# A chunked state-space scan: running sums made once and spread by DMA, decays made one head pair ahead

## The reference, cut to what matters

```python
acs = jnp.cumsum(dt * a.reshape(G, R), axis=2)          # running sums inside chunks of 128
xdt = x * dt[..., None]
seg = at[..., :, None] - at[..., None, :]               # at = acs with time last
decay = jnp.exp(jnp.where(causal, seg, -jnp.inf))       # 128 x 128 per head and chunk
cb = jnp.einsum('bctgn,bcsgn->bcgts', cm, bm)
y_diag = jnp.einsum('bcgrts,bcsgrp->bctgrp', cb[:, :, :, None] * decay, xdt)
decay_s = jnp.exp(acs[:, :, -1:] - acs)
states = jnp.einsum('bcsgn,bcsgr,bcsgrp->bcgrpn', bm, decay_s, xdt)
...
y_off = jnp.einsum('bctgn,bcgrpn,bctgr->bctgrp', cm, h_in, jnp.exp(acs))
```

## Time and profile before

| | before |
|---|---|
| median of 3 runs | 2653.37 us (2649.86 to 2658.57) |
| span of the profiled execution | 2654.9 us (its own time is not listed apart from the span) |
| TensorE matmul / weight load | 2539.5 us (96%) / 2452.5 us (92%) |
| VectorE | 1279.4 us (48%) |
| ScalarE | 728.7 us (27%) |
| GpSimd | 532.4 us (20%) |
| instructions | 46230 |
| bytes read / written in HBM | 207.20 MB / 14.49 MB |

### The profile page before, as it was taken

One profiled execution on the slowest core, in us unless ns is written; L12 is line 12 of the kernel. 1 busy time (PEld: TensorE's weight loads), 2 busy tenths in 40 slices (PEclk: granted clock), 3 DMA queues, 4 the chain that ended last, 5 costly groups with the idle time before them and its releaser, 6 DMA issues.

```text
span 2654.9 us, 46230 instructions
## 1 busy us (share of the span) xinstructions
PE 2539.5 (96%) x18319; PEld 2452.5 (92%) x18319; DVE 1279.4 (48%) x1499; ACT 728.7 (27%) x1016; POOL 532.4 (20%) x388
## 2 busy tenths in 40 slices
PE   7999999898989879999999999999999999999997
PEld 7999999887878668999999999999998989999997
DVE  5434334778677776343433244434325635344323
ACT  4222222321212223222222232222224533222212
POOL 1000022456556552300000210000123222000021
PEclk9999999999999888999999999999999979999999
DMA  3222224122232221222222222222222102222222
GB/s 121 83 83 79 88 87 137 56 89 90 90 101 93 82 73 62 79 86 81 79 87 85 89 80 79 86 80 79 90 93 89 40 26 80 87 79 82 85 89 81
DMA packets 61268, 220.47 MB, mean 83 GB/s; under 512 B 7120, under 2 KB 7248, under 8 KB 61056
## 3 DMA queue, kind: packets, MB, share of 16 engines
q1 hardware_dynamic: 52560, 187.72, 20.8%
q0 software_dynamic: 8368, 31.59, 3.9%
q10 hardware_dynamic: 288, 0.44, 0.0%
HBM read 207.20 MB, written 14.49 MB: 84 GB/s over the span
## 4 chain that ended last, share of the span: by engine, by line
PE 89%; DVE 5%; issue 3%; ACT 1%; DMA 1%; POOL 0%; DVEq 0%; ACTq 0%; POOLq 0%
PE psum L383 71%; PE psum L401 6%; PE psum L552 1%; PE psum L580 1%; DVE cacc L1192 1%; PE psum L666 1%; PE psum L573 1%; PE psum L548 1%; DVE xdd L1299 1%; PE psum L749 1%; PE psum L536 1%; PE psum L677 1%; PE psum L689 0%; PE psum L529 0%; DVE ylo L1413 0%
## 5 line engine op out<-in xcount | busy, mean ns | idle before, releaser
L1088 DVE TENSOR_TENSOR wlo<-wraw,whi 128x1024 fp32r<-128x1024 f32 x342 | 439.0, 1284 | 987.1 <-ACT whi L800 987.1
L383 PE MATMUL psum<-xhi,whi 128*128 128x288 f32 x3152 | 681.0, 298 | 21.9 <-DVE xlo L1094 15.1
L383 PE MATMUL psum<-xhi,wlo 128*128 128x288 f32 x3152 | 677.6, 297 | 0.0
L383 PE MATMUL psum<-xlo,whi 128*128 128x288 f32 x3152 | 677.5, 297 | 0.0
L800 ACT ACTIVATE whi<-wraw 128x1024 fp32r<-128x1024 f32 x349 | 369.8, 1059 | 973.0 <-PE psum L383 936.1
L383 PEld LDWEIGHTS psum<-xhi,whi 128*128 128x128 f32 x3152 | 510.8, 190 | 26.5 <-issue 21.9
L383 PEld LDWEIGHTS psum<-xlo,whi 128*128 128x128 f32 x3152 | 510.9, 190 | 0.0
L383 PEld LDWEIGHTS psum<-xhi,wlo 128*128 128x128 f32 x3152 | 510.4, 190 | 0.0
L383 PE MATMUL psum<-hhi,whi 128*128 128x288 f32 x1408 | 302.7, 296 | 0.0
L383 PE MATMUL psum<-hlo,whi 128*128 128x288 f32 x1408 | 302.7, 296 | 0.0
L383 PE MATMUL psum<-hhi,wlo 128*128 128x288 f32 x1408 | 302.7, 296 | 0.0
(11 more groups left out here) (258 smaller groups left out, 2892.7 us busy)
## 6 DMA issues: line engine op xcount, KB each, us to landing
wraw<-w SPq DMA_DIRECT2D x349, 512.0 KB, 3.2
h0s<-ssm_state POOLq DMA_DIRECT2D x16, 512.0 KB, 4.7
h0T<-ssm_state_t POOLq DMA_DIRECT2D x16, 512.0 KB, 5.0
ssm_s<-h0s POOLq DMA_DIRECT2D x16, 512.0 KB, 3.8
x<-x_in SPq DMA_DIRECT2D x8, 288.0 KB, 7.1
y<-ybuf SPq DMA_DIRECT2D x8, 288.0 KB, 2.5
kv_kept<-cache_kv POOLq DMA_DIRECT2D x1, 1920.0 KB, 8.9
ssm_p<-hst POOLq DMA_DIRECT2D x16, 64.0 KB, 1.9
```

The lines of the kernel that those rows point to most:

```text
L383: last = pe.matmul(acc[:, 2 * pair + half, 0:HALF], wt[s][:, k * P:(k + 1) * P], m[:, k0 + k, half * HALF:(half + 1) * HALF], start=start ...
L1088: dve.tensor_tensor(wlo[n % 2][:], wraw[n % 2][:], whi[n % 2][:].bitcast(F32), ALU.subtract).then_inc(weights_lo, 1)
```

## The change

The running sums of dt * a are made once, for all heads, by eight small matmuls between the B/C products of groups 0 and 1 (`cumulate`), once with heads on partitions (`arow`) and once with time on partitions (`acol`), together with the samples' decay to the end (`dend`). `arow` is stored in a scratch tensor in HBM, and for each pair a DMA of GpSimd's queue reads its two rows into all 128 partitions (`A`, 576 KB). ScalarE makes E from A with a Relu of (acol - A) per head and chunk and one Exp of scale -1 over all, and E2 with two Exp from A; E and E2 have two buffers each, and this is done for p+1 in body p, between `split_hi` and `hT`. The segment products, their operands on GpSimd and the constants for them are gone. `Bm` has half the columns, with 32 partitions per product. The loops over bodies are written out on TensorE, ScalarE, VectorE and GpSimd.

```diff
+            def cumulate():
+                pe.wait_ge(dt_kept, 2)
+                for c in range(NC):
+                    pe.matmul(bank[5][0:HEADS, c * L:(c + 1) * L], dT[:, c, HEADS:], tri, start=True, stop=True)
+                pe.matmul(bank[6][0:HEADS, 0:S], dT[0:S, NC, HEADS:], tri_s, start=True, stop=True)
+                pe.matmul(bank[7][:, 0:NC * HEADS], tri, dT[:, 0:NC, HEADS:], start=True, stop=True)
+                pe.matmul(bank[7][0:S, 128:128 + HEADS], tri_s, dT[0:S, NC, HEADS:], start=True, stop=True)
+                pe.matmul(bank[7][0:S, 192:192 + HEADS], strict_s, dT[0:S, NC, HEADS:], start=True,
+                          stop=True).then_inc(cum_done, 1)
...
                     if g == 1:
-                        pe.wait_ge(dt_kept, 4)
+                        cumulate()
+                        pe.wait_ge(cum_kept, 5)
...
-            def decays(p, first):
+            def turn_x(p, first):
...
-                pe.wait_ge(seg_lhs, 3 * p + 3)
...
-                for h in range(2):
-                    for part, seg in enumerate((seghi, seglo)):
-                        pe.matmul(bank[2 + h][:, :], strict_r[:], seg[:, h, :, :].rearrange("p c t -> p (c t)"),
-                                  start=part == 0, stop=part == 1)
...
             def states(p, g):
-                pe.wait_ge(decay_ready, 5 * p + 5)
                 pe.wait_ge(xdd_ready, 2 * p + 2)
+                if p:
+                    pe.wait_ge(h_step, 4 * p)
+                    pe.wait_ge(ss_final, p)
...
                 for b in range(2):
-                    last = pe.matmul(bank[3 + b][:, :], xdd[0:S, NC, :], Bm[:, 4 * b:4 * b + 4, :], start=True, stop=True)
+                    half = slice(b * S // 2, (b + 1) * S // 2)
+                    last = pe.matmul(bank[3 + b][:, :], xdd[half, NC, :], Bm[half], start=True, stop=True)
...
+            def keep_cumulated():
+                act.wait_ge(cum_done, 1)
+                act.activation(arow[:, 0:SEQ], bank[5][0:HEADS, :], ACT.Copy).then_inc(cum_kept, 1)
+                act.activation(arow[:, SEQ:T], bank[6][0:HEADS, 0:S], ACT.Copy).then_inc(cum_kept, 1)
...
+            def exponentials(p):
+                e, e2 = E[p % 2], E2[p % 2]
+                act.wait_ge(a_loaded, 16 * p + 16)
+                if p >= 2:
+                    act.wait_ge(ssd_done, p - 1)
+                    act.wait_ge(y_step, 5 * (p - 2) + 3)
+                    act.wait_ge(h0_decayed, p - 1)
                 for h in range(2):
...
+                    for c in range(NC):
+                        act.activation(e[:, h, c * L:(c + 1) * L], A[:, h, c * L:(c + 1) * L], ACT.Relu,
+                                       bias=acol[:, c, 2 * p + h:2 * p + h + 1], scale=-1.0).then_inc(gap_ready, 1)
+                    act.activation(e[0:S, h, SEQ:T], A[0:S, h, SEQ:T], ACT.Relu,
+                                   bias=acol[0:S, NC, 2 * p + h:2 * p + h + 1], scale=-1.0).then_inc(gap_ready, 1)
+                for h in range(2):
+                    rows = slice(h * HEAD_DIM, (h + 1) * HEAD_DIM)
+                    act.activation(e2[rows, :], A[rows, h, :], ACT.Exp).then_inc(e2_ready, 1)
+                act.wait_ge(gap_ready, 2 * (NC + 1) * (p + 1))
+                act.wait_ge(e2_ready, 2 * p + 2)
+                act.activation(e[:], e[:], ACT.Exp, scale=-1.0).then_inc(e_ready, 1)
...
                 def body(p, first=False, more=True, stats=None):
-                    exponentials(p, first)
                     if more:
                         split_hi(n + 3, 2 * p)
+                        exponentials(p + 1)
...
-                    dve.wait_ge(decay_ready, 5 * p + 3)
+                    dve.wait_ge(e_ready, p + 1)
...
+            def load_rows(p):
+                pool.dma_start(A[:], cum_rows[2 * p:2 * p + 2, :].unsqueeze(0).to_broadcast([P, 2, T])).then_inc(a_loaded, 16)
...
                     if more:
-                        pool.wait_ge(seg_ready, p + 1)
-                        seg_operands(p + 1)
+                        if p + 2 < NX:
+                            pool.wait_ge(e2_ready, 2 * p + 4)
+                            load_rows(p + 2)
                         keep_rows(p + 1, p + 1 + 2 * GROUPS, m + 2 * p + 1)
...
                 keep_rows(0, 2 * GROUPS, m)
-                pool.wait_ge(dt_kept, 4)
-                seg_operands(0)
+                pool.wait_ge(cum_kept, 2)
+                pool.wait_ge(conv_done, 4 * GROUPS)
+                pool.dma_start(cum_rows, arow[:]).then_inc(rows_stored, 16)
+                pool.wait_ge(rows_stored, 16)
+                load_rows(0)
                 pool.wait_ge(b_kept, 2 * GROUPS)
                 sequence_b(0, first=True)
-                body(0, 0, first=True)
-                with pool.Fori(1, 4) as p:
-                    body(p, 0)
...
+                pool.wait_ge(e2_ready, 2)
+                load_rows(1)
+                for p in range(NX):
+                    if p % 4 == 0 and p:
+                        sequence_b(p // 4)
+                    body(p, p // 4, first=p == 0, more=p < NX - 1, finish=p - 13 if p > 12 else None)
```

More of the change, by code:

```diff
@@ L149, in build @@
         cbm = mam("cbm", [P, GROUPS, T])
-        Bm = mam("Bm", [S, DEC_BATCH, P])
-        E = mam("E", [P, 2, ES])
-        E2 = mam("E2", [P, T])
+        Bm = mam("Bm", [S, DEC_BATCH // 2, P])
+        E = [mam(f"E{s}", [P, 2, T]) for s in range(2)]
+        E2 = [mam(f"E2{s}", [P, T]) for s in range(2)]
         xdt = mam("xdt", [P, NC + 1, P])
@@ L520, in decays, with states @@
                 pe.transpose(bank[7][0:S, 0:P], xs[:, SEQ:T], ident).then_inc(x_turned, 1)
-                pe.wait_ge(seg_lhs, 3 * p + 3)
-                if not first:
+            def states(p, g):
+                pe.wait_ge(xdd_ready, 2 * p + 2)
+                if p:
                     pe.wait_ge(h_step, 4 * p)
-                if not first:
                     pe.wait_ge(ss_final, p)
-                for h in range(2):
-                    for part, seg in enumerate((seghi, seglo)):
-                        pe.matmul(bank[2 + h][:, :], strict_r[:], seg[:, h, :, :].rearrange("p c t -> p (c t)"),
-                                  start=part == 0, stop=part == 1)
[L531 to L543, removed]
-                pe.wait_ge(decay_ready, 5 * p + 5)
-                pe.wait_ge(xdd_ready, 2 * p + 2)
                 for c in range(NC):
@@ L593, in body @@
                         half_unit(n + 1, 0, 0, 1)
-                    decays(p, first)
+                    turn_x(p, first)
                     if more and not first:
@@ L618, in heads @@
                 b_c_products()
-                pe.wait_ge(consts_r, 2)
-                body(0, 0, first=True)
-                with pe.Fori(1, 4) as p:
-                    body(p, 0)
[L623 to L628, removed]
+                for p in range(NX):
+                    body(p, p // 4, first=p == 0, more=p < NX - 1, stats=p - 12 if 12 <= p < NX - 1 else None)
             def group_sum(g, b):
@@ L929, in heads @@
                 conv_act(2 * GROUPS)
[L930 to L935, removed]
+                exponentials(0)
+                for p in range(NX):
+                    body(p, first=p == 0, more=p < NX - 1, stats=p - 12 if 12 <= p < NX - 1 else None)
             def group_std(g):
@@ L986, in exponentials @@
                         act.activation(esink[:, h, :], nmax[:, h, :], ACT.Exp,
-                                       bias=acol(SINK, head)).then_inc(p_exp, 1)
+                                       bias=att_col(SINK, head)).then_inc(p_exp, 1)
                 def out_hi(j):
@@ L1368, in heads @@
                 conv_out(xs, 2 * GROUPS)
-                body(0, 0, first=True)
-                with dve.Fori(1, 4) as p:
-                    body(p, 0)
-                with dve.Fori(1, GROUPS - 1) as g:
-                    with dve.Fori(0, 4) as q:
-                        body(g * 4 + q, g)
-                body(12, GROUPS - 1, stats=0)
-                with dve.Fori(1, GROUPS - 1) as q:
-                    body(q + 12, GROUPS - 1, stats=q, finish=q - 1)
-                body(NX - 1, GROUPS - 1, more=False, finish=GROUPS - 2)
+                for p in range(NX):
+                    body(p, p // 4, first=p == 0, more=p < NX - 1, stats=p - 12 if 12 <= p < NX - 1 else None,
+                         finish=p - 13 if p > 12 else None)
             def group_var(g, b):
```

130 lines of the change are left out of this document (44 added, 86 removed).

## The result

The changed kernel takes 2596.99 us (median of 4 runs, 2588.82 to 2600.86) against 2655.9 (2649.86 to 2658.57) for the kernel before on the same chip: a ratio of 0.977, 95% interval 0.975 to 0.980. The profiled execution spans 2595.2 us against 2654.9. The forecast, 2604, is 7 us above the time.

The account below looks back on a forecast made before the run. TensorE, 89% of the chain, was taken to bound the kernel. Ordinary bodies -22, groups' first bodies -33, last three -2 and the start +5.4 made -52 us from 2655, forecast as 2604, range 2580 to 2658.

Parts of the forecast that it names:

- Who wins between VectorE and GpSimd: Ordinary scan bodies: the two engines hand over at each instruction, L1299 ending at t=8.0, a gain of 2.5 us; chance 0.40.
- rival Q: Ordinary bodies: VectorE keeps its turn from L1297 to L1299, xdd at 6.7, body 21.9 us; total 2589, chance 0.25.
- The suspicion that the string at p=4 began with the product on 64 partitions: At p=4, GpSimd's five-instruction string blocking VectorE for 8.22 us began with L1642 on 64 partitions, unlike ordinary bodies' full-width operations.
- R: GpSimd keeps VectorE off through three instructions; TensorE idles 3.7 us per body, ordinary bodies 30.3; +32, 2687, chance 0.15.
- Ordinary bodies, 22.2 on average for 23.3: Nine ordinary scan bodies fall from 25.8 to 23.3 us, 2.5 each, -22 us in all.
- Part 1: Segment products leave TensorE in the scan: -2.9 us per body.
- Part 3: ScalarE makes E one pair ahead in a block of 6.4 us, hidden with 1.8 us to spare.
- Part 4: Rows spread by a 576 KB transfer with 16 us available at the floor; it fits, so costs nothing.
- Part 5: Loops become straight code: zero; bounds a gain of some tenths per body and a loss of a few us in all.
- Part 6: Start of the scan: small fp32 matmuls, ScalarE copies and later E delay xdd by +5.4 us; bounds +4 and +18.
- Groups' first bodies, 24.6 to 25.5: Bodies p=4, 8, 12: weight split waits behind three GpSimd instructions to t=12; gain 11 us each, 33 in all.
- Last three, -2: Last three bodies: waits for GpSimd's gated products and the reciprocal stay; L1299's 1.7 us block at p=14 goes: -2 us.

Follow-up runs that it names:

- experiments 1 and 2: Changed kernel with Bm over all 128 rows: 2576.5 us; changed kernel with a tiny GpSimd product added per body: 2646.3 on 64 rows, 2593.6 on 128.
- experiment 8: Kernel before with only its loops over head pairs written out as straight code: 2659.8 us against 2656.6, ratio 1.0015.
- experiment 6: Changed kernel with the last three bodies' group norm moved: 2559.4 us; second kernel adding Bm over all rows and GpSimd held for xdd: 2556.0.
- experiment 4: Changed kernel with the removed TensorE products put back, their result unused: 2590.5 us, ratio 0.976.
- 128-row control: Changed kernel with a tiny unread GpSimd product over 128x8 elements added ahead of L1609 in each body: 2593.6 us, ratio 0.978.

## Why the prediction was right, and where its steps were not

- **The time.** Against the span of 2654.9 the forecast took 51.6 us off, and 59.7 went. The ordinary bodies gave 13.1 more than forecast and the start cost 0.8 less; the first bodies of the groups gave 2.4 less, the last three 1.3 less, and the rest of the execution was 2.1 longer. The mechanism was right, but that the total came within 8 us is partly that these offset each other.
- **Who wins between VectorE and GpSimd.** Right: L1285 ended at t=7.7 (forecast 8.0; rival Q had 6.7), and in ordinary bodies L1283 starts right behind xdt, where L1297 waited 2.59 us for E. The suspicion that the string at p=4 began with the product on 64 partitions is confirmed by experiments 1 and 2. That nothing on 64 partitions stands ahead of L1609 in ordinary bodies is why R did not happen; R itself was real, priced 2687, measured 2646: its ordinary bodies took 28.4 us and not 30.3, and p=4, 8, 12 took 30 us less than before, not 14.
- **Ordinary bodies, 22.2 on average for 23.3.** Before, two of the nine were longer than the 25.8 taken for all (p=10 26.6, p=11 27.2), which adds 2.4 us to the gain. The rest is two terms. The states were to take what L548 and L552 took; the pair of half-height products takes 1.13 for 1.98, a part of the diff (32 rows each) that the forecast did not price: -0.85. And the weight split L1079 was taken to wait out the h0s product; it went first in most, as rival Q's evidence had it, so L547 started at t=13.2 and not 14.7. Four of the nine (22.6 to 22.7) lost 0.8 to 0.9 of this again.
- **Part 1, -2.9 us per body.** The step that failed, though the total hid it. As a floor for one body it is right; as a gain of the edit it is not: the products back cost 1.7 us in an ordinary body and nothing measurable in all (2590.5 to 2597.0). The products, the half-height pair, the lead of one pair and the loops were each tried and are worth nothing clear of noise alone. What is left as the cause is that xdd no longer waits for segment products and exponentials, and that GpSimd's string is shorter. That is by elimination and by the traces; no run put a late E or GpSimd's operands back, so the share of each is not shown.
- **Part 3.** The block takes 5.45 us, not 6.4, and is hidden. A Relu by itself takes 0.39 us as forecast, but four in a row take 1.26, since they overlap. The lead of one pair is not what hides it: ScalarE idles 9.05 us ahead of its split, and the block fits there.
- **Part 4.** Right: the 576 KB land in 4.2 us (median), and no ordinary body waits for them.
- **Part 5.** Zero was taken; it is +3 (1.5 parts in a thousand).
- **Part 6, +5.4.** In size right (+4.6 for p=0), by other terms. The first states start 6.8 us later after the first b/c transposes than before. One reason is the clock of this execution, 0.54 and 0.55 over the b/c products from 521 to 528 and 528 to 536 us; another is that L1283 took 3.19 us, 2.5 more than by itself, which no step foresaw. With the b/c products at 2.4 GHz on both sides the first states start 19.8 us after the first transposes in the kernel before (experiment 8's execution) and 24.2 in the changed one (experiment 6, first kernel, which has the same block and the same 3.19 us): +4.4.
- **Groups' first bodies, 24.6 to 25.5.** Measured 27.0, 25.9, 27.7. The forecast had the weight split wait behind three GpSimd products; L1168 ahead of it waited for them too, and the evictions came late: TensorE idled 2.48 us for them, and the body's mean clock was 0.87 at p=4.
- **Last three, -2.** Near (-0.7), and blind to the chance: with E early the reciprocal L1367 is what xdd waits for at p=13. Moving it and the four products is worth 26 us in these bodies and 37.6 in the median (experiment 6).

## What to carry to other kernels

An engine's work that fills another engine's wait is worth nothing when removed; find the wait that ends last, take that out first, and price the work again afterwards: here the same products cost nothing measurable and then 19 us. Where VectorE and GpSimd run side by side, look at which instruction each long one waited for, and let GpSimd's operations cover all 128 partitions even where half would do. After an edit makes one operand early, read what its consumer waits for next in every kind of body, the last ones too.

## What the runs showed of the hardware

- A GpSimd instruction on 64 partitions costs as much as on 128 (1.09 and 1.08 us for 512 columns), and a waiting VectorE instruction did not get in between the full-height ones that follow it without a gap: the 64x128 product took 4.64 us, against 0.29 with the 128-row control. The Trainium skill (GPSIMD Engine Reference, 2.1 Instruction dispatch) says that each of eight cores serves 16 partitions and begins the next instruction when its own share is done. That would fit, if half of them run ahead and the shared port is never free; this is a guess, no run here looks at single cores. The rule of the Trainium skill (SBUF — State Buffer, Who interferes with whom) that the later engine is blocked until the first one's instruction finishes agrees with the waits behind full-height instructions in ordinary bodies (1.50 and 1.11 us). It does not agree with those behind a 64-partition one (4.64 and 3.98 us) and at p=0 (3.19 us).
- At p=0 two full-height instructions right behind a DMA issue also held VectorE for both (3.19 us), with Bm on 64 or on 128 rows. Whether the issue is the cause was not tried.
- Two TensorE products of 512 columns on different 32 rows take 1.13 us together, on the same 32 rows, or on 64 rows each, 1.98. The Trainium skill (TensorE: Matmul & The Clock Gate, Part 3: Packing small matmuls) says that small products placed on different rows of the array run at the same time; the traces agree.
- The states took 1.16 us in a body after an idle of 0.65 and 2.08 after one of 3.8, and from p=1 on the stage's mean granted clock rose from 0.90 to 0.96 when the needless products of experiment 4 were added.
